# Two-layer hybrid block: feed-forward inputs turned unnormed, the row factor applied behind gate and up

## The reference, cut to what matters

```python
def _rmsnorm(x, g):
    y = xf * lax.rsqrt(jnp.mean(xf * xf, axis=-1, keepdims=True) + RMS_EPS)
    return (y * g).astype(x.dtype)
def _swiglu(x, wg, wu, wd):
    return (jax.nn.silu(x @ wg) * (x @ wu)) @ wd
for layer in range(DEPTH):                      # DEPTH = 2
    h = h + 0.5 * _swiglu(_rmsnorm(h, norm_ffn1[layer]), ...)   # D_FF = 2816
    h = h + mixer(_rmsnorm(h, norm_mix[layer]))  # 0: attention + convolution, 1: recurrent
    h = h + 0.5 * _swiglu(_rmsnorm(h, norm_ffn2[layer]), ...)
return _rmsnorm(h, norm_final)
```

## Time and profile before

| | us |
|---|---|
| median of 3 runs (1664.5 to 1671.64) | 1666.43 |
| span of the profiled execution | 1667.5 |
| TensorE busy | 1438.0 (86%) |
| VectorE busy | 922.9 (55%) |
| ScalarE busy | 684.2 (41%) |
| GpSimd busy | 35.3 (2%) |

### The profile page before, as it was taken

One profiled execution on the slowest core, in us unless ns is written; L12 is line 12 of the kernel. 1 busy time (PEld: TensorE's weight loads), 2 busy tenths in 40 slices (PEclk: granted clock), 3 DMA queues, 4 the chain that ended last, 5 costly groups with the idle time before them and its releaser, 6 DMA issues.

```text
span 1667.5 us, 24874 instructions
## 1 busy us (share of the span) xinstructions
PE 1438.0 (86%) x9548; PEld 1117.0 (67%) x9548; DVE 922.9 (55%) x1759; ACT 684.2 (41%) x1238; POOL 35.3 (2%) x48
## 2 busy tenths in 40 slices
PE   7987866678977656799999689999899998899998
PEld 6865432356654323588887468888788888778886
DVE  5674211157741111666667857666666668766666
ACT  5371110144711001544441445555555446664443
POOL 0000000001000000100000000000000000000000
PEclk9998987998989888899999989999999999999999
DMA  9818999995289999955554224455455453455510
GB/s 390 331 58 347 387 428 428 428 428 217 90 346 402 427 428 428 417 197 202 187 202 163 107 101 167 187 201 201 152 202 201 178 200 128 176 190 202 181 71 26
DMA packets 31614, 408.65 MB, mean 245 GB/s; under 512 B 3456, under 2 KB 5632, under 8 KB 7216
## 3 DMA queue, kind: packets, MB, share of 16 engines
q1 hardware_dynamic: 29088, 404.34, 61.1%
q10 hardware_dynamic: 2448, 3.24, 0.6%
HBM read 406.50 MB, written 1.06 MB: 244 GB/s over the span
## 4 chain that ended last, share of the span: by engine, by line
PE 70%; DMA 15%; DVE 9%; ACT 4%; issue 1%; POOL 1%; DVEq 0%; SPq 0%; POOLq 0%; ACTq 0%
PE bank L1813 20%; DMA ring<-stream 15%; PE bank L1817 10%; PE bank L1845 9%; PE bank L670 5%; PE bank L1851 4%; PE bank L1589 3%; PE bank L1607 3%; PE bank L676 2%; PE bank L611 2%; PE bank L1967 2%; PE bank L638 1%; PE bank L1520 1%; DVE near_both L461 1%; PE bank L2023 1%
## 5 line engine op out<-in xcount | busy, mean ns | idle before, releaser
L529 DVE TENSOR_TENSOR unit_lo<-ring,unit_hi 128x1024 fp32r<-128x1024 f32 x324 | 394.4, 1223 | 253.6 <-ACT unit_hi L524 253.2
L524 ACT ACTIVATE unit_hi<-ring 128x1024 fp32r<-128x1024 f32 x324 | 341.8, 1062 | 376.5 <-PE bank L1817 251.5
L1813 PE MATMUL bank<-near_both,unit_hi 128*128 128x512 f32 x1408 | 360.0, 396 | 3.0 <-DVE near_both L461 2.7
L1813 PEld LDWEIGHTS bank<-near_both,unit_hi 128*128 128x128 f32 x1408 | 256.7, 188 | 61.8 <-DVE near_both L461 4.8
L1817 PEld LDWEIGHTS bank<-near_both,unit_lo 128*128 128x128 f32 x1408 | 187.3, 188 | 16.1
L1817 PE MATMUL bank<-near_both,unit_lo 128*128 128x256 f32 x1408 | 189.7, 277 | 0.0
L1589 PE MATMUL bank<-ring,work 128*32 128x256 f32 x1792 | 121.7, 424 | 55.0 <-DMA ring<-stream 55.0
L1589 PEld LDWEIGHTS bank<-ring,work 128*32 128x32 f32 x1792 | 59.5, 119 | 112.9 <-DMA ring<-stream 71.8
L1845 PE MATMUL bank<-unit_hi,act_hi 128*128 128x512 f32 x336 | 131.3, 391 | 0.0
L1845 PE MATMUL bank<-unit_hi,act_lo 128*128 128x512 f32 x336 | 131.2, 390 | 0.0
L1751 DVE TENSOR_TENSOR work<-work,bank 128x128 f32<-128x128 f32 x32 | 9.2, 288 | 165.4 <-ACT work L1661 165.4
(11 more groups left out here) (312 smaller groups left out, 1909.3 us busy)
## 6 DMA issues: line engine op xcount, KB each, us to landing
ring<-stream SPq DMA_DIRECT2D x180, 2048.0 KB, 12.2
work<-ahead SPq DMA_DIRECT2D x4, 2048.0 KB, 10.1
ahead<-ahead SPq DMA_DIRECT2D x4, 2048.0 KB, 18.0
kept_slot<-ahead SPq DMA_DIRECT2D x2, 2048.0 KB, 23.9
ring<-stream SPq DMA_DIRECT2D x4, 512.0 KB, 7.5
work<-spread ACTq DMA_DIRECT2D x2, 1024.0 KB, 13.5
x<-x_in SPq DMA_DIRECT2D x2, 512.0 KB, 4.5
work<-final_rows ACTq DMA_DIRECT2D x2, 512.0 KB, 7.7
```

Source lines behind the costliest of these rows:

```text
L524: nc.scalar.activation(high_buf(name, u), raw_unit(name, u), ACT.Copy).then_inc(hi_done, 1)
L529: low = nc.vector.tensor_tensor(low_buf(name, u), raw_unit(name, u), high_buf(name, u).bitcast(F32), ALU.subtract)
L1813: nc.tensor.matmul(out[:, :], high[:, k, :], near_both[:, :, KD - 1 - k, :], start=(k == 0), stop=False, skip_group_check=True)
```

## The change

- `norm_pe` is gone from the four feed-forward inputs. `raw_turn_pe` turns one quarter of `x` itself, as soon as its add is done: 4 transposes. The turns stand inside the output product of the stage before where two quarters are ready (`s_out`, `r_out`, ffn1), or right behind it.
- The row factor is turned too (`scale_turn_pe`: two transposes of the broadcast factor into bank 1), copied by ScalarE to `row_scale` (`scale_act`), and multiplied by VectorE into gate and up as they leave PSUM (`scaled`). The squares for it (`raw_norm_act`, `raw_norm_dve`: two quarters on each engine) run beside the transposes.
- `hidden` makes two products of 256 columns for each of 512; so one PSUM half holds everything, and the second half's copy and add are gone.
- The first tile makes gate and up together (`first_hidden`): all products that need only the high part of a group, then those by the low part, in the order in which the parts come.
- For ffn0, `final_norm` is folded into the column gain (one multiply at the start, 8 more parameter columns), the weighted squares are formed from `x` squared times `final_norm` squared, and POOL restores `x` by two multiplies and two scalings.
- Order: VectorE multiplies gate before it splits the next up unit, and splits the down unit after the products; the next stage's early splits are spread about the last tile's sums or stand at the end of the mixers. The last tile of ffn1 goes by `HALVES`.

```diff
+        def raw_turn_pe(pe, name, i):
+            t = HALVES[i][0]
+            quarter_ready(pe, RAW[name], i)
+            for j in (2 * (i // 2), 2 * (i // 2) + 1):
+                g = TURN_AT[name][0] + j
+                for src, at, rows, cols in TURNS[g][0][t::2]:
+                    last = nc.tensor.transpose(split_bank(name, g)[0:rows, at:at + cols], src, ident)
+                if t == 1:
+                    last.then_inc(turned, 1)
+        def scale_turn_pe(pe, name):
+            at = ZR + 2 if name == "n4" else RS
+            pe.wait_ge(power_out, POWERS["f0" if name == "n4" else name] + 1)
+            for t in range(NT):
+                mm = nc.tensor.transpose(bank[1][:, t * P:(t + 1) * P], stat[:, at + t:at + t + 1].to_broadcast([P, P]), ident)
+            mm.then_inc(scale_turned, 1)
...
             def hidden(f, u, which, it):
-                    nc.tensor.matmul(out[:, :], high[:, k, :], near_both[:, :, KD - 1 - k, :], start=(k == 0), stop=False,
-                                     skip_group_check=True)
+                    nc.tensor.matmul(out, high[:, k, :], near(near_hi, k), start=(k == 0), stop=False)
+                    nc.tensor.matmul(out, high[:, k, :], near(near_lo, k), start=False, stop=False)
...
+                if name in ("ffn0", "ffn2"):
+                    for i in range(0 if name == "ffn0" else 2, 4):
+                        raw_turn_pe(pe, turns, i)
...
+                    for j in range(4):
+                        by_high(j)
+                    for j in range(4):
+                        by_low(j)
+                    return
+                raw_turn_pe(pe, turns, 2)
...
+                by_high(0)
+                raw_turn_pe(pe, turns, 3)
+                by_high(1)
+                by_low(0)
+                by_low(1)
+                by_high(2)
+                by_high(3)
+                by_low(2)
+                by_low(3)
...
-            gate_up(0)
+            first_hidden()
+            if name != "ffn0":
+                scale_turn_pe(pe, turns)
...
+        def raw_norm_dve(v, name, early=0):
...
+            for i in (2, 3):
+                t, cols = HALVES[i]
+                quarter_ready(v, p, i)
+                nc.vector.tensor_tensor_reduce(W[:, 512 * i:512 * i + 512], x[:, t, cols], x[:, t, cols], 1.0 / D, 0.0,
+                                               ALU.mult, ALU.add, stat[:, SS + i:SS + i + 1]).then_inc(sq_dve, 1)
...
+            for j in range(early, 4):
+                split_evac(v, 1, name, j)
...
+            def scaled(f, which, it=0):
+                u, out = (up_unit(f), up_f) if which else (gate_unit(f), silu_f)
+                v.wait_ge(unit_used, UNIT_BASE[name] + u + 1 + PASS_UNITS * it)
+                nc.vector.tensor_tensor(out[:, f % 2, :], hidden_bank(f, which)[:, 0:T], row_scale,
+                                        ALU.mult).then_inc(ffn_scaled, 1)
...
+            def tile(f, it=0):
+                split_low(v, name, gate_unit(f + 1), it)
+                if f == 0:
+                    v.wait_ge(scale_out, 1 + sorted(RAW).index(FFN_TURNS[name]))
+                scaled(f, 0, it)
+                split_low(v, name, up_unit(f + 1), it)
+                scaled(f, 1, it)
+                product(f, it)
+                split_low(v, name, down_unit(f), it)
```

More of the change, by code:

```diff
@@ new lines, in square @@
+                nc.scalar.activation(x_sq[i], x[:, t, cols], ACT.Square, scale=D ** -0.5,
+                                     accum_out=stat[:, ZX + i:ZX + i + 1]).then_inc(sq_act, 1)
+            act.wait_ge(final_in, 16)
+            nc.scalar.activation(rows_sq, rows, ACT.Square).then_inc(rows_squared, 1)
+            square(0)
+            square(1)
+            for u in range(EARLY):
+                split_high(act, "ffn0", u)
+            for j in range(4):
+                split_evac(act, 0, "n4", j)
@@ new lines, in double_norm_act, with weighted_sum @@
+            square(2)
+            square(3)
+        def double_norm_dve(v):
+            def weighted_sum(i):
+                cols = HALVES[i][1]
+                v.wait_ge(sq_act, SQUARES[4][0] + i + 1)
+                nc.vector.tensor_tensor_reduce(x_sq[i], x_sq[i], rows_sq[:, cols], 1.0, 0.0, ALU.mult, ALU.add,
+                                               stat[:, ZZ + i:ZZ + i + 1]).then_inc(sq_dve, 1)
+            for u in range(EARLY):
+                split_low(v, "ffn0", u)
+            v.wait_ge(rows_squared, 1)
+            weighted_sum(0)
+            weighted_sum(1)
+            for j in range(4):
+                split_evac(v, 1, "n4", j)
+            weighted_sum(2)
+            weighted_sum(3)
+            v.wait_ge(sq_dve, SQUARES[4][1] + 4)
@@ L1797, in hidden_bank, with parts @@
         def hidden_bank(f, which):
-            return bank[4 + 2 * (f % 2) + which]
+            return bank[5 - f % 2 + 2 * which]
         def ffn_pe(pe, i):
             base, name = FT * i, f"ffn{i}"
-            turns = TURN_AT[FFN_TURNS[name]][0]
+            turns, first = FFN_TURNS[name], TURN_AT[FFN_TURNS[name]][0]
+            def parts(u):
+                return (half(name, u).rearrange("p (k c) -> p k c", k=KD) for half in (high_buf, low_buf))
             def hidden(f, u, which, it):
-                out = hidden_bank(f, which)
-                high = high_buf(name, u).rearrange("p (k c) -> p k c", k=KD)
-                low = low_buf(name, u).rearrange("p (k c) -> p k c", k=KD)
+                out = hidden_bank(f, which)[:, 0:T]
+                high, low = parts(u)
@@ L2080, in s_mix_act @@
                 split_high(act, "s_out", u)
+            for u in range(EARLY):
+                split_high(act, "ffn1", u)
         def s_mix_dve(v):
@@ L2267, in r_gates_act @@
                 split_high(act, "r_out", u)
+            for u in range(EARLY):
+                split_high(act, "ffn3", u)
         def r_mix_dve(v):
@@ L2353, in r_mix_dve @@
                 split_low(v, "r_out", u)
+            for u in range(EARLY):
+                split_low(v, "ffn3", u)
             residual_add(v, "r_out")
```

284 lines of the change are left out of this document (145 added, 139 removed).

## The result

| | before | after |
|---|---|---|
| median of the runs, us | 1669.04 (4 runs beside it) | 1656.01 (1653.32 to 1656.42, 4 runs) |
| span of the profiled execution, us | 1667.5 | 1654.6 |
| one steady feed-forward tile, us | 8.293 | 8.373 |

The ratio is 0.9916, 95% interval 0.9896 to 0.9936: the change takes 13 us off, where 32.3 were forecast. 1656 lies above the range, beyond rivals B and C.

What follows compares the result with a forecast made beforehand. TensorE's own instructions were taken to pace each tile. Gains of 10.0 (stream), 5.7 (ffn0), 4.5 (ffn1), 7.2 (ffn2), 4.1 (ffn3) and 0.8 (exit of ffn2) summed to 32.3 us, giving 1634 us; range 1625 to 1648.

Steps and rivals of the forecast that it cites:

- Rival B: Splitting saves nothing because both halves pay a fixed part: gain 22.3 us, 1644 (1648 by the page's rule); chance 0.13.
- Rival C: Feed-forward entrances stay at half clock after pauses of some 2 us: 7.2 us back, 1641; chance 0.14.
- What bounds the kernel: Feed-forward tiles: TensorE's own instructions pace them, busy 8.29 of 8.29 us; 88 tiles are some 730 us.
- So gate and up become 2.72 each and the tile 8.17: Steady tiles: split products at 113 ns, as in the recurrent loop, save 0.12 us in each of 83 tiles, 10.0 us.
- The bounds, 0 to 11.6: Range in us given to the tile stream's gain, from 2.78 staying to 0.14 saved a tile.
- The page's rule: Warm product costs N/2.4 + 2.5 ns, so splitting loses 2.5 ns each, 3.5 us in all; set against the stream gain.
- ScalarE and VectorE in a tile, at nothing: Steady tiles: their new work costs nothing, hidden by TensorE with slack of 6 us or more; VectorE stays 5.44 us busy.
- rival D: TensorE waits for VectorE in every tile; 0.5 us a tile gives 9 us slower, 1676; chance 0.04.
- ffn1, ffn2, ffn3: Entrances of these feed-forwards: gains of 4.5, 7.2 and 4.1 us as tile 1's gate starts earlier.
- Exit of ffn2, 0.8: End of ffn2: with two splits no longer ahead, the adds finish 0.8 us earlier, gain 0.8.
- POOL's restore grows...; x is wanted only at 873, so nothing: Entrance of ffn0: two added multiplies of 1024 columns on POOL cost nothing; the entrance gains 5.7 us.

Runs made afterwards that it cites:

- b_split_last: Kernel before, two-piece 512-column products split into two of 256, last product of each down block halved, one start flag a bank: 1661.18 us, ratio 0.9951.
- b_split: Kernel before with only each two-piece 512-column product of the hidden tiles split into two of 256: 1676.98 us, ratio 1.0044.
- a_restore_late: Kernel after the change, GpSimd's restoring of x in ffn0 made to wait until behind the first down block: 1651.16 us.
- a_restore_dveb: Kernel after the change, restoring of x moved from GpSimd to VectorE, four operations in tiles 18 and 19 of ffn0: 1650.33 us.
- best: Kernel after the change, last product of each down block halved and restoring of x moved to VectorE: 1636.24 us, ratio 0.9804.
- a_first_apart: Kernel after the change, first tile's gate and up run one behind the other after all turned groups are awaited: 1675.62 us, ratio to before 1.0047.
- a_down256: Kernel after the change, every 512-column product of a down block (except a stage's last block) split into two of 256: 1648.99 us.

## Why the prediction was wrong, step by step

- **What bounds the kernel**: right. TensorE fills every tile before and after.
- **"So gate and up become 2.72 each and the tile 8.17"**: this is the step that failed, by 16.6 of the 19.3 us that are missing. 8.373 was measured, +6.6 us and not -10.0. The recurrent rows are the same loop and did run at 113.3 ns, but I took the duration of an operation without looking at what ran ahead of it. There it was transposes and other 256-column products. In a tile a down block of 512-column products stands ahead, and behind it the same products take 117.7. The kernel before held a hint: gate's low-weight products took 115 ns a piece because the first three started 121, 116 and 114 ns apart, and only the rest 113. With one halved product the step yields most of what was forecast: 8.200 for 8.17, b_split_last -7.9 us for -10.0.
- **The bounds, 0 to 11.6**: wrong, since they shut out a loss. A split adds an instruction, and nothing I had shown excluded that both halves run slower together than the whole: 2 x 117.7 = 235.4 against 233.4 ns in gate and 232.7 in up, and each low-weight product 3 to 4 more (117.8 for 114.8 and 114.0). Rival B was near in kind; its bottom was set too high.
- The page's rule which I set against this (the Trainium skill, TensorE: Matmul & The Clock Gate, "Back-to-back issue gap") had the right sign; it is given there for single products. By 2.5 ns a split it makes 3.5 us of loss by an estimate; b_split lost 6.8. The 2.0 and 2.7 ns a pair are near it and make 3.2 us; the low-weight products, which were not split, add 4.6, and down gives 1.2 back. But the agreement is chance or holds for one pace only: in b_split_last a pair takes 226.7 ns, 6 less than the whole.
- **ScalarE and VectorE in a tile, at nothing**: right. DVE is busy 5.62 us of 8.37 (5.44 told), ACT 3.49, and no wait in a steady tile; rival D did not come.
- **ffn1, ffn2, ffn3**: right or cautious. 7.7, 7.5 and 7.7 us from last product to gate(1) where 8, 7 and 8 were told. In ffn1 and ffn3 that is 5.8 us less than before, and the 8 transposes ahead of the last product (0.9) bring the gain to 4.9, for 4.5 and 4.1; in ffn2 7.2, less 0.4 for its transposes, for 7.2. The other 2.2 us of ffn1's stretch are within the scatter given under the table.
- **Exit of ffn2, 0.8**: about right. The transposes follow the last product by 3.07 us for 3.83, as told, and r_in's first product by 6.39 for 8.23. Then r_in runs at clock 0.65 from its first product to the second unit's low-weight products (6.96 us), where before it had 1.00 (5.55). To the end of r_in's first unit it is 11.5 us for 12.0, so 0.5 is gained. This clock is not the change's own: a_restore_late, with the same program here, ran the unit at full clock (11.5 becomes 10.1), and b_split, with the exit of the kernel before, ran it at half (12.0 becomes 13.5). The windows of after, before, a_restore_late and b_split, one after another:

```profile
1373.33:1380.29 6.96, 6.96 (x40) 6.96 (x41) 6.13 (x15) 4.46 (x7) 0.00 (x0) 0.65 0.00 0
```

```profile
1384.68:1390.23 5.55, 5.46 (x41) 4.86 (x41) 5.14 (x9) 3.28 (x5) 0.00 (x0) 1.00 0.00 0
```

```profile
1374.00:1377.70 3.70, 3.60 (x24) 3.02 (x25) 3.32 (x7) 3.29 (x5) 0.00 (x0) 1.00 0.00 0
```

```profile
1389.20:1394.40 5.20, 5.20 (x25) 5.20 (x26) 4.82 (x8) 3.29 (x5) 0.00 (x0) 0.51 0.00 0
```

- **ffn0, "POOL's restore grows...; x is wanted only at 873, so nothing"**: wrong, 3.9 us short. The result is not wanted early, but GpSimd's work holds up VectorE while tile 0's activations hang on it. Against a_restore_dveb, down(0)'s wait is 2.4 us longer (2.92 for 0.49), an earlier one for L542 0.3 (0.56 for 0.23), and down(0) itself takes 1.6 more at half clock: with 0.35 us of smaller shifts, the 4.7 between the two. From the scatter's end to down(0)'s end it is 23.4 us in after; with the restoring gone from there 18.8 in best, for 19.5 told. The rows here show only operations with both inputs in SBUF stretched (L2010, L2013, L542), while L2001, with one input in PSUM, kept its 0.41 us. That fits a rule I should have weighed: the Trainium skill (SBUF — State Buffer, "SBUF: two separate sides") says that a VectorE operation with two SBUF inputs and a GpSimd operation that reads SBUF shut each other out for a whole instruction. The trace agrees for the two multiplies: L2010 took 2.15 us and ended at 700.53, 0.28 us behind the GpSimd multiply beside it (row below), and in a_restore_late both stretched multiplies end 0.28 us behind one too. It does not agree for the two scalings (L1043): beside them L2013 takes 1.14 us and three splits (L542) from 701.96 on take 1.21, 1.21 and 1.80, so two of them were not held up at all.

```profile
696.89 3.35 POOL L1040 TENSOR_TENSOR x<-x,work 128x1024 f32<-128x1024 f32 x1
```

- **Rival C**: false in ffn1 to ffn3, true once in ffn0 (at down(0), not at its first products) and everywhere in a_first_apart. Its "pauses of some 2 us" were 2.23 us at the old ffn1 and ffn3, but 3.47 at ffn2 and 6.22 at ffn0.

The forecast of 1634 comes near the kernel named best, 1636, not the change as it was made; and near it in part because a tile of 8.20 for 8.17 is made up for by ffn0's entrance, 0.7 us better than told, and ffn3's, 0.8.

## What to carry to other kernels

Take the duration of a product from a row with the same neighbours, not only the same shape, and after each edit of a dense stream look whether the untouched products changed too: 4.4 ns on each of 48 products in 83 tiles is 17 us here. When an instruction is split, let the range reach to a loss. Work that is "hidden" on GpSimd can hold up VectorE's SBUF operations, here by 4.7 us; put it where VectorE's own idle time can take it, and price each added wait of TensorE twice, once for itself and once for the clock behind it.

## What the hardware showed that I had not expected

- One and the same 256-column product is issued every 113.3 or every 117.7 ns at full clock. The long pace lasts through six units of r_in, 144 products, in after; and in the tiles the next 512-column block ends the short one: its first three products take 232 ns, the rest 227, and the 48 behind it 117.7. A last product in two halves (113, then 119 to 122 for three) brings the short pace back; a 16-column product ahead of the gate does not, nor does the order of addresses. In r_in the same program ran at 113.3 in one execution and at 117.7 in another. Why is open: no view here shows the inside of TensorE's queue.
- 24 products of 256 columns in the down block, in pairs on the same weights, took 119 ns each in the mean in the kernel where the gate's ran at 113.3 (a_down256).
- Two splits on VectorE with both inputs in SBUF kept their 1.21 us beside GpSimd's scalings (L1043, 3.15 and 3.54 us), while beside a GpSimd multiply of 3.35 us (L1040) a VectorE multiply of 0.42 us took 2.15.
